# Three 2 MB weight transfers dealt as 112, 7, 7 and 2 rows instead of 128

## What is computed

```
gu = (hb @ w_gate_up[e] + b_gate_up[e]).astype(jnp.float32)
gate, up = gu[:, :D_EXPERT], gu[:, D_EXPERT:]
gate = jnp.minimum(gate, SWIGLU_LIMIT)
up = jnp.clip(up, -SWIGLU_LIMIT, SWIGLU_LIMIT)
act = (up + 1.0) * (gate * jax.nn.sigmoid(SWIGLU_ALPHA * gate))
return (act.astype(x2d.dtype) @ w_down[e] + b_down[e]).astype(jnp.float32)
```

## Time and profile before

| | us |
|---|---|
| median of three runs | 1221.45 |
| the profiled execution | 1221.28 |
| its span, first to last instruction | 1219.3 |
| TensorE matmuls busy | 1180.4 (97%) |
| VectorE busy | 392.8 (32%) |
| ScalarE busy | 226.5 (19%) |
| GpSimd busy | 82.7 (7%) |
| HBM read | 440.63 MB, 363 GB/s over the span |

### The profile page before, as it was taken

One profiled execution on the slowest core, in us unless ns is written; L12 is line 12 of the kernel. 1 busy time (PEld: TensorE's weight loads), 2 busy tenths in 40 slices (PEclk: granted clock), 3 DMA queues, 4 the chain that ended last, 5 costly groups with the idle time before them and its releaser, 6 DMA issues.

```text
span 1219.3 us, 16213 instructions
## 1 busy us (share of the span) xinstructions
PE 1180.4 (97%) x6479; PEld 670.6 (55%) x6479; DVE 392.8 (32%) x665; ACT 226.5 (19%) x390; POOL 82.7 (7%) x244
## 2 busy tenths in 40 slices
PE   8999999999999999899998989999999998999997
PEld 7999999985535354334434343535535343553533
DVE  4648586753343423021211111111212111121213
ACT  5533673133101010101101010101001010110102
POOL 4100000010201001101000010101011010110000
PEclk9999999999999999999999999999999999999999
DMA  7543226598999999999999999999999999999995
GB/s 231 171 158 109 98 105 241 184 342 350 429 424 428 426 427 425 425 427 425 424 429 426 425 425 421 421 424 425 427 429 426 425 426 428 427 426 427 425 424 223
DMA packets 54736, 443.71 MB, mean 364 GB/s; under 512 B 5340, under 2 KB 5436, under 8 KB 23680
## 3 DMA queue, kind: packets, MB, share of 16 engines
q1 hardware_dynamic: 53296, 439.91, 87.4%
q0 software_dynamic: 1216, 2.68, 0.9%
q10 hardware_dynamic: 144, 0.04, 0.0%
HBM read 440.63 MB, written 1.98 MB: 363 GB/s over the span
## 4 chain that ended last, share of the span: by engine, by line
PE 86%; DMA 10%; issue 1%; DVE 1%; POOLq 0%; ACT 0%; POOL 0%; ACTq 0%; DVEq 0%; SPq 0%
PE ps L1724 32%; PE ps L1792 18%; DMA wexp<-in_w_gate_up_dram 10%; PE ps L1616 7%; PE ps L1355 7%; PE ps L1357 7%; PE ps L1356 7%; PE ps L1632 2%; PE ps L1633 1%; PE ps L1666 1%; PE ps L1461 1%; PE ps L1736 1%; PE ps L1624 1%; DMA rows<-in_conv_w_dram 1%; PE ps L1578 0%
## 5 line engine op out<-in xcount | busy, mean ns | idle before, releaser
L1724 PE MATMUL ps<-wexp,xt 128*64 128x512 f32 (+1 forms) x2048 | 462.4, 602 | 16.6 <-DMA wexp<-in_w_gate_up_dram 11.1
L1724 PEld LDWEIGHTS ps<-wexp,xt 128*64 128x64 f32 (+1 forms) x2048 | 144.2, 132 | 262.1 <-issue 261.7
L1792 PE MATMUL ps<-wexp,act_t 128*64 128x512 f32 (+1 forms) x1104 | 227.0, 593 | 4.2 <-issue 4.2
L1792 PEld LDWEIGHTS ps<-wexp,act_t 128*64 128x64 f32 (+1 forms) x1104 | 82.0, 131 | 134.2 <-issue 134.1
L1259 DVE TENSOR_TENSOR y<-y,ps 128x1024 f32<-128x1024 f32 x51 | 60.8, 1219 | 209.8 <-PE ps L1633 201.0
L825 ACT ACTIVATE g<-g 128x512 f32<-128x512 f32 x33 | 20.8, 630 | 546.2 <-DVE g L1273 546.2
L1355 PE MATMUL ps<-act_h,split 128*128 128x384 f32 x352 | 117.9, 335 | 0.0
L1357 PE MATMUL ps<-act_h,split 128*128 128x384 f32 x352 | 117.6, 334 | 0.0
L1356 PE MATMUL ps<-act_l,split 128*128 128x384 f32 x352 | 117.6, 334 | 0.0
L1616 PEld LDWEIGHTS ps<-pick,xn 128*128 128x128 f32 x768 | 91.1, 196 | 14.8 <-issue 14.8
L1616 PE MATMUL ps<-pick,xn 128*128 128x128 f32 x768 | 94.1, 283 | 1.7 <-POOL pick L588 1.7
(11 more groups left out here) (327 smaller groups left out, 972.6 us busy)
## 6 DMA issues: line engine op xcount, KB each, us to landing
wexp<-in_w_gate_up_dram SPq DMA_DIRECT2D x92, 2048.0 KB, 24.7
wexp<-in_w_down_dram SPq DMA_DIRECT2D x48, 2048.0 KB, 26.3
wexp<-in_w_gate_up_dram SPq DMA_DIRECT2D x38, 1024.0 KB, 25.5
wexp<-in_w_down_dram SPq DMA_DIRECT2D x20, 1024.0 KB, 12.5
raw<-in_w_in_dram SPq DMA_DIRECT2D x19, 1024.0 KB, 5.1
wexp_low<-in_w_gate_up_dram SPq DMA_DIRECT2D x17, 1024.0 KB, 24.1
wexp_high<-in_w_gate_up_dram SPq DMA_DIRECT2D x16, 1024.0 KB, 23.4
wexp_low<-in_w_down_dram SPq DMA_DIRECT2D x5, 1024.0 KB, 21.2
```

Source lines behind the costliest of these rows:

```text
L1724: i_ = pe.matmul(ps[s0:s0 + w, b, :], xt[:, k, s0:s0 + w], weights(k, x)[:, at_:at_ + UC], start=k == 0, stop=k == CB - 1)
L1792: i_ = pe.matmul(ps[s0:s0 + w, 6 + c, :], act_, weights(CB + m, x)[:, D * kk + UC * c:D * kk + UC * c + UC], start=k == 0, stop=k == CB - 1)
```

## The change

In `load_pass`, three transfers of 2048 KB are issued as four. They are the third of passes 7, 10 and 12 (place `PLACES[p] + 4`, n = 4, m = 1, x = 0): the gate-up rows of steps k = 2 and 3 of the first expert of the pair. The first 112 rows raise the slot's semaphore as before; rows 112 to 119, 119 to 126 and 126 to 128 raise a new semaphore, `spread_landed`, by 16 each. TensorE waits for it, besides the old ones, at step k = 2 of those passes, for 48, 96 and 144.

```
+SPREAD = tuple(PLACES[p_] + 4 for p_ in (7, 10, 12))
+SPREAD_ROWS = 112
+SPREAD_PIECES = ((112, 119), (119, 126), (126, 128))
...
+        spread_landed = sem("spread_landed")
...
+                    if unit + n - 1 in SPREAD:
+                        rows_ = exp_two(ids[x], m)
+                        sp.dma_start(wtwo[slot // 2][0:SPREAD_ROWS], rows_[0:SPREAD_ROWS]).then_inc(exp_landed[slot], 16)
+                        for r0, r1 in SPREAD_PIECES:
+                            sp.dma_start(wtwo[slot // 2][r0:r1], rows_[r0:r1]).then_inc(spread_landed, 16)
+                        continue
                     sp.dma_start(wtwo[slot // 2][:], exp_two(ids[x], m)).then_inc(exp_landed[slot], 16)
...
+                        if place(k, x) in SPREAD:
+                            pe.wait_ge(spread_landed, 16 * len(SPREAD_PIECES) * (SPREAD.index(place(k, x)) + 1))
                         slot, count = place(k, x) % RINGS, 16 * landings(place(k, x))
```

## The result

| | before | after |
|---|---|---|
| median, us (runs) | 1221.43 (4) | 1258.11 (4) |
| lowest and highest, us | 1221.22 to 1223.68 | 1254.13 to 1263.83 |
| profiled execution, us; its span | 1221.28; 1219.3 | 1254.13; 1252.1 |

The changed kernel is slower: ratio 1.0302, interval 1.0283 to 1.0320, 36.7 us between the medians and 32.8 us between the two spans. The forecast was slower by 9.6 us, with 1240 us as the upper end of its range. The sign was right, and the size was off by more than three times. The profiled execution is the fastest of the four, so the trace accounts for 32.8 us and not for the last 4 us of the difference between the medians.

What follows compares the result with a forecast made beforehand. The DMA engines' pace sets the last awaited weight landing, followed by a fixed tail. Each split costs +2.3 and +0.9 us, +9.6 for three: 1221.3 + 9.6 = 1230.9, plus 0.2 for the median, 1231.0 us; range 1219.3 to 1240.

Steps and rivals of the forecast that it cites:

- What bounds the kernel: Whole kernel: the end is the weight landing at 1154.62 us, set by the DMA engines' pace, plus a fixed tail.
- Issue and TensorE's waits: 0: At the three splits: nine more issues are covered by the queue and three added TensorE conditions cost nothing.
- The gain's account, -1.85 us: In the split transfers: nine late engines get seven rows instead of eight, saving 0.615 us three times, 1.85 us in all.
- The 112-row part: Each split's large transfer: its seven rows an engine run at 0.60 of the pace, 7.2 us instead of 4.9, +2.3 us.
- The upper bound, +16.5 us: Three splits: two engines at half pace on all seven rows, +3.7 us, and small transfers at twice their price, +1.8 us.
- The small ones: Each split's 16 remaining rows, 256 KB, priced as twice a small transfer of 0.45 us: +0.9 us.
- How it plays out: TensorE's waits: at 708.66 us from 2.75 to about 6 us, at 1006.55 from 1.09 to about 7.5; end slips 9.6.
- The clock: After longer TensorE waits: granted clock may fall to 0.50, costing 1.7 us each, which the next wait for weights swallows.
- The signs that were named: Profile after: DMA rate well below 424 GB/s for 5 to 15 us per split, engines busy; few engines finish last loads late.
- Relief of the late nine: Rival at the 1154.62 us landing: nine late engines are relieved and nothing meets, -1.85 us, 1219.6 us; chance 0.28.
- its cancelling: Rival at the splits: relief and meeting of rows cancel, or buffers hide all of it, 1221.4 us; chance 0.09.
- The sixteen rows all on one engine: Rival at the splits: pieces go to one engine, 23 rows instead of 8, about 1241 us; chance 0.03.

## Why the prediction was right in sign and wrong in size

*What bounds the kernel.* Right. The end moved by what the landing in the last chain moved, 32.81 us of 32.8. The runs with one split say so more sharply: a loss at 380 us or in the stretch where weights lie ready is paid in full at the end.

*Issue and TensorE's waits: 0.* Right, by the cut into columns (ratio 1.0000): the same nine issues and three conditions.

*The gain's account, -1.85 us.* It did not come in any run. The 112 rows alone, with 16 rows left out and so less to move for the engines together, cost 28.8 us. The account was built on how many rows an engine has to move. Where every row takes 1.2 us instead of 0.6, that number no longer sets the end; whether a gain of this size lies hidden in the loss, no run separates.

*The 112-row part: "7 x 0.615 / 0.60 = 7.2 us instead of 4.9, +2.3 us".* **This is the step that failed.** The 112 rows alone cost 9.6 us a split, not 2.3. Two things were wrong with it. The smaller one is the pace: 0.60 from the earlier trace rows, with little else under way, where in the full stream it was half or less, 170 to 233 GB/s. The larger one is whose time I slowed. I let the odd rows run slowly and everybody else at full pace. But all rows of all engines were slow together, 0.85 us and more instead of 0.61, so ordinary transfers of 128 rows ran at half pace too: a 2048 KB transfer landed 40.1 us after its issue instead of 31.3. The windows give the size of it. From 675 to 695 us, 5 x (233 + 193 + 203 + 170) = 3995 KB are moved, about twice the 2.1 MB of the split transfer; at full pace they would take 9.4 us, so 10.6 are lost. The earlier trace rows held the hint: four small transfers brought the whole stream from 406 to 316 GB/s for 7 us, and I charged that loss to the small ones as a fixed price each, instead of asking for how many bytes the whole stream is slow.

*The upper bound, +16.5 us.* It was none. It put half pace on the odd rows alone. Half pace on them and on as many bytes of others is 2 x 4.92 = 9.8 us a split and 29.5 us for three, near the 32.8 of the span.

*The small ones: +0.9 us a split.* Measured 2.6, loosely; it is the smaller term, as said.

*How it plays out.* The mechanism held and the positions were off. The wait at the end of pass 7 was to grow to 6 us; it stayed at 2.76, and 7.72 and 2.63 us came ahead of it. The first wait of pass 12 was to be 7.5 us; a wait of 8.00 came earlier, at 974.77. The clock, as the text had it, fell behind the larger waits (0.50 from 685 to 690 us), which is the 1.2 GHz level, and cost nothing by itself, since the next wait for weights takes it up: the end followed the landing.

*The signs that were named.* The rate well below 424 GB/s with the engines counted busy: it came, for 20 to 25 us rather than 5 to 15. One or few engines running long after the others at the end: rather a slope over some 7 us.

*Rivals.* Relief of the late nine and its cancelling both fell, for the reason above. The sixteen rows all on one engine was to give about 1241 us; since the 112 rows alone give 1251, it has nothing left to explain. The packets speak against it as well: the page after counts 5388 packets under 512 B against 5340, 48 more for the nine small pieces. With one small packet for each engine that a piece is dealt to, as above, that is 3 x (7 + 7 + 2), a row to an engine; on one engine each, the pieces would have left nine. So the pieces were dealt as they divide, as the forecast had it; which engines took them the trace does not name.

**What stays open.** If only the odd transfer's own 4.9 us were doubled, a split would cost 4.9 us and not 9 to 12. The rest is the time in which some engines are in the split rows and others not yet or no longer, and in which all are slow alike (the packets under the two halves of 64 rows). Why an engine that is in an ordinary transfer is slowed at once, and by a factor of two, is not shown; that engines stalled at a foreign place hold the others up would do it, but no run tests it. The runs with all 2 MB cut by neighbouring rows give 9.1 to 11.5 us a split, the full change 12.2 from its medians and 10.9 from its spans; what the last few us are made of was not taken apart. No variant beat the kernel before; those with evenly spread rows only equal it.

## What to carry to other kernels

In a saturated stream of DMA, ask of each transfer which rows of SBUF it writes, before you ask how many: a 2 MB transfer in parts whose rows crowd into half of the places, or come out at seven for each engine, cost 9 to 12 us here, and the same bytes over every second or fourth row, or over all 128 rows in column pieces, cost nothing. If a transfer must be cut, cut it by columns. When you price something that shares a resource, price what everybody loses: read the fall of the whole rate and its length in a row like the earlier trace rows, and do not charge it to the newcomer alone. And a bound is one only if it also lets the neighbours be slow.

## What the runs showed of the hardware that was not expected

- The rate in the dips is about half whether a transfer has 64, 32 or 16 rows in the crowded places (216 to 223, 210 to 223, and 241 to 262 GB/s over ten us with the dip's edges in them), where it is 422 to 433 with the rows spread.
- In the dip every row is slow, also those of ordinary transfers: 192 rows of 16 KB from 675 to 690 us took 0.85 to 1.78 us each, where 392 took 0.61 to 0.63 before.
- The DMA engines' busy share tells little of it: 0.92 to 1.07 in the first dip of the changed kernel, and 0.87 to 1.08 in that of the split in pass 2. The rate beside it does.
- Which rows of DRAM are read did not matter (1221.94 us with the sources in halves).
- A split early in the program (380 us), where TensorE does not wait for weights, cost 9.1 us of the end, nearly as much as one in pass 7.
